# Attention rounds: the first score block moves between the values and the first transposes, the third behind the fourth portion of GEMM products

## The reference

```python
def even_mixer(...):   # layer 0: two kinds of heads, outputs side by side
    o_a, _ = banded_attention(qa, ka, va, slopes_a, 127, 1, sinks)  # 8 heads, softmax over a band
    o_b = stick_breaking_attention(qb, kb, vb)                      # 8 heads, sigmoids and a product
    return concatenate([o_a, o_b]) @ w_out
def odd_mixer(...):    # layer 1: 16 heads, dilated patterns, softmax
def dsa_sparse_attention(...):   # layer 2: 16 heads, softmax over selected keys
```

## Time and profile before

| what | value |
|---|---|
| time, median of 3 (lowest to highest) | 3058.09 us (3057.76 to 3059.72) |
| the profiled execution's own time | 3058.59 us |
| its span | 3056.8 us |
| TensorE busy | 3039.6 us, 99% of the span |
| VectorE, ScalarE, GpSimd busy | 2035.4, 1416.4, 450.1 us |
| stage EV | about 447 to 542 us |
| stage OC | about 1559 to 1652 us |
| stage SX | about 2528 to 2622 us |
| a round of SX, between two starts of first transposes | 11.72 us (2540.14 to 2551.86) |

### The profile page before, as it was taken

One profiled execution on the slowest core, in us unless ns is written; L12 is line 12 of the kernel. 1 busy time (PEld: TensorE's weight loads), 2 busy tenths in 40 slices (PEclk: granted clock), 3 DMA queues, 4 the chain that ended last, 5 costly groups with the idle time before them and its releaser, 6 DMA issues.

```text
span 3056.8 us, 44796 instructions
## 1 busy us (share of the span) xinstructions
PE 3039.6 (99%) x17960; PEld 2621.2 (86%) x17960; DVE 2035.4 (67%) x2896; ACT 1416.4 (46%) x2189; POOL 450.1 (15%) x550
## 2 busy tenths in 40 slices
PE   9999999999999999999999999999999999999999
PEld 8998886887999899988867879998887786789987
DVE  7886258755888478863565757886336876578873
ACT  6444247544444344442455545444236727454442
POOL 1112014212110011101310212110152200031100
PEclk9999999999999999999999999999999999999999
DMA  7763330423774267633232416763332231247732
GB/s 210 175 164 98 102 97 29 146 69 99 193 178 138 97 151 180 162 114 99 88 96 77 152 49 160 178 163 113 86 99 83 79 108 35 76 112 187 170 117 70
DMA packets 287360, 366.93 MB, mean 120 GB/s; under 512 B 12304, under 2 KB 211344, under 8 KB 287024
## 3 DMA queue, kind: packets, MB, share of 16 engines
q1 hardware_dynamic: 233392, 304.42, 31.4%
q0 software_dynamic: 53184, 59.32, 11.9%
q10 hardware_dynamic: 576, 0.33, 0.0%
HBM read 361.92 MB, written 2.10 MB: 119 GB/s over the span
## 4 chain that ended last, share of the span: by engine, by line
PE 94%; issue 3%; POOL 1%; DVE 1%; ACT 1%; POOLq 0%; DVEq 0%; ACTq 0%
PE ps L94 91%; PE ps L97 3%; POOL evQ L142 1%; ACT wh L100 0%; POOL evPb L142 0%; DVE hTl L109 0%; POOL evPa L142 0%; DVE wl L103 0%; DVE xT L103 0%; DVE evQ L115 0%; DVE s_gb L103 0%; POOL rc L103 0%; ACT u_R L100 0%; ACT xn L100 0%; POOL c0ss L103 0%
## 5 line engine op out<-in xcount | busy, mean ns | idle before, releaser
L103 DVE TENSOR_TENSOR wl<-raw,wh 128x1024 fp32r<-128x1024 f32 (+2 forms) x485 | 596.6, 1236 | 498.0 <-ACT wh L100 493.7
L100 ACT ACTIVATE wh<-raw 128x1024 fp32r<-128x1024 f32 (+2 forms) x485 | 504.8, 1049 | 808.7 <-PE ps L94 768.2
L94 PE MATMUL ps<-hTh,wh 128*128 128x256 f32 (+1 forms) x2016 | 671.1, 333 | 2.4 <-DVE wl L103 1.7
L94 PE MATMUL ps<-hTh,wl 128*128 128x256 f32 (+1 forms) x2016 | 666.9, 331 | 0.0
L94 PE MATMUL ps<-hTl,wh 128*128 128x256 f32 (+1 forms) x2016 | 625.0, 331 | 0.2 <-DVE hTl L109 0.2
L94 PEld LDWEIGHTS ps<-hTh,wh 128*128 128x128 f32 x2016 | 383.7, 190 | 44.5 <-issue 9.2
L94 PEld LDWEIGHTS ps<-hTh,wl 128*128 128x128 f32 x2016 | 383.8, 190 | 38.1 <-issue 7.5
L94 PEld LDWEIGHTS ps<-hTl,wh 128*128 128x128 f32 x2016 | 382.6, 191 | 37.4 <-issue 4.7
L100 ACT ACTIVATE wh<-u_raw 128x1024 fp32r<-128x1024 f32 x190 | 201.4, 1062 | 299.9 <-PE ps L94 281.9
L94 PE MATMUL ps<-u_Fh,wl 128*128 128x512 f32 x704 | 273.9, 389 | 0.0
L94 PE MATMUL ps<-u_Fh,wh 128*128 128x512 f32 x704 | 273.9, 389 | 0.0
(11 more groups left out here) (423 smaller groups left out, 6106.3 us busy)
## 6 DMA issues: line engine op xcount, KB each, us to landing
raw<-in_ffn_w_gu SPq DMA_DIRECT2D x118, 512.0 KB, 4.7
raw<-in_ffn_w_down SPq DMA_DIRECT2D x88, 512.0 KB, 3.6
u_raw<-in_ffn_w_gu SPq DMA_DIRECT2D x77, 512.0 KB, 4.9
raw<-in_ffn_w_gu POOLq DMA_DIRECT2D x40, 512.0 KB, 6.1
u_raw<-in_ffn_w_gu POOLq DMA_DIRECT2D x38, 512.0 KB, 6.1
raw<-in_xa_w_kv SPq DMA_DIRECT2D x32, 512.0 KB, 3.7
raw<-in_w_in SPq DMA_DIRECT2D x28, 512.0 KB, 3.6
raw<-in_od_w_in SPq DMA_DIRECT2D x24, 512.0 KB, 3.8
```

The source lines that it names most:

```text
L94: return self.made(lambda e: e.matmul(*a, **k))
L100: return self.made(lambda e: e.activation(*a, **k))
L103: return self.made(lambda e: e.tensor_tensor(*a, **k))
```

## The change

Two calls in TensorE's order move. Nothing else in the program changes: the orders of the other engines, the tiles, the banks, the portions of products and all computed values stay.

```diff
@@ -1244,8 +1244,8 @@
         fill(-1, 3)
         fill(-1, 4)
         for g in range(T_.N):
+            scores(g + 1, 0)
             turn(g, 0, slice(0, 1))
-            scores(g + 1, 0)
             fill(g, 0)
             turn(g, 0, slice(1, None))
             fill(g, 1)
@@ -1257,9 +1257,9 @@
                 turn(g, 1, slice(0, 1))
                 fill(g, 2)
                 turn(g, 1, slice(1, -1))
-            scores(g + 1, 2)
             if g + 1 == T_.N or len(T_.seq[g + 1][0].groups) == 3:
                 fill(g, 3)
+                scores(g + 1, 2)
                 turn(g, 1, slice(-1, None))
             else:
                 turn(g, 1, slice(-1, None))
```

## The result

The changed kernel takes 3069.09 us (median of 6 executions, 3068.51 to 3070.98), the kernel before beside it 3058.38 (6, 3057.76 to 3059.72). The ratio is 1.0036, interval 1.0026 to 1.0046: 10.7 us slower. 3066.1 was forecast, with 3059 to 3072 as the range and 0.77 on "slower". The profiled execution took 3068.58 us, its span is 3066.8.

A forecast was written before the change was run, and what follows sets the result against it. TensorE, busy for 3039.6 of 3056.8 us, was taken as the bound. OC and SX +6.8 and EV +1.6 gave 8.4, said as 8.0, on 3058.1: 3066.1 us, range 3059 to 3072.

The forecast's parts named there:

- The order's saving: TensorE's order in a round: two mode changes for three; head 0's six transposes at 2.01 and not 2.22, saving 0.21.
- first edit: Score block 0 ahead of the first transposes: saves 0.21 by order, but ScalarE's copy comes 1.11 later and a wait appears.
- step from values straight into scores: TensorE at a round's start: entering the score form from values costs between nothing and 0.23; taken as 0.05.
- The wait: Before head 1's transposes: the late copy delays exponentials and division to 5.30, a new wait of 0.79 in every round.
- Rival (a): Only TensorE's own order counts and ScalarE's exponentials hold nothing up: 6 us saved, 3052; chance 0.07.
- the margin: In an OC round, from the first division's end at 4.19 to head 1's transposes at 4.73: 0.54.
- The sum: OC and SX 6.8 plus EV 1.6 give 8.4 us slower; 8.0 said.
- EV, the term that was mis-sized: EV stage: banded rounds 0 to 2 +1.3, round 3 -0.6, stick-breaking rounds 4 to 6 +0.9; +1.6 in all.
- The second edit: Score block 2 behind the fourth portion: saves about 0.1 a round and covers VectorE's late drain of its bank.
- rival (d): The new waits pull the granted clock down, half clock for some 3 us in 14 rounds: 3087; chance 0.07.

The follow-up runs named there:

- e3: Both edits as in the changed kernel, plus two of head 1's four exponentials moved early on ScalarE; 3056.96 us, ratio 0.9995 to the kernel before.
- e10: Both edits as in the changed kernel, plus one of head 1's exponentials moved early on ScalarE; 3062.82 us, ratio 1.0015 to the kernel before.
- e6: Kernel before with score block 2 moved and two GEMM products ahead of the first transposes in rounds 1 to 6 of OC and SX; 3058.84 us.
- after: The changed kernel, with both edits against the kernel before; 3069.09 us, ratio 1.0036.
- e1: Kernel before with only score block 0 moved ahead of the first transposes, score block 2 at its old place; 3074.87 us, ratio 1.0056.
- b1: The kernel before, unchanged and profiled once more; 3057.20 us (one execution).
- e2: Kernel before with only score block 2 moved behind the fourth portion, first transposes right behind the values; 3058.74 us, ratio 1.0001.
- e9: Kernel before with two early exponentials, score block 0 moved in softmax rounds only, score block 2 in OC and SX only; 3055.37 us, ratio 0.9991.
- e8: Both edits and two early exponentials, but score block 0 unmoved in stick-breaking rounds, score block 2 unmoved in OC and SX round 3; 3056.78 us, ratio 0.9996.

## Why the prediction was right, and where its sizes were off

**The order's saving.** 0.21 a round was forecast for the first edit. With the wait taken away (e3), a round is 11.42 and not 11.63: 0.21. The Trainium skill, TensorEngine Tiling (Array Packing), Key Properties, has each change of mode drain TensorE; one change fewer did pay, 0.21 in e3. The step from values straight into scores, taken at 0.05 with 0.23 as its upper end, cost nothing: values to scores is 2.30 (1582.69 to 1584.99), as values to transposes was the earlier trace rows.

**The wait.** The round followed the forecast nearly row by row, from the values' end: ScalarE's copy at 1.76 (forecast 1.81), the division's end at 5.26 (5.30), head 1's transposes at 5.41 (5.36), 0.87 later than score block 1 would let them start (0.79; the profile's own figure for the wait, 0.80, is counted from a modelled end), score block 2 at 7.80 (7.75) without a wait, the values at 9.97 (9.89), the end at 12.27 (12.19). e3 and e10 show that the wait is this chain's. Rival (a) needed a delay under the margin; it was 1.06, for 0.54 by the prediction and 0.39 by e6.

**Who ended the wait.** I wrote that the transposes start 0.06 behind the division, which would be 5.32. They start at 5.41, and for OC and SX the profile names ScalarE's `ocPT` copy, whose merged row ends at 1589.42 + 0.91 = 1590.33, 0.07 earlier. That name misleads. By the kernel's two alternating banks, head 1's first transposes take the bank of head 0's second group, and only the first two of the three copies read it. In a narrower window they end at 1589.42 + 0.64 = 1590.06, 0.34 ahead of the transposes:

```profile
1589.42 0.64 ACT L100 ACTIVATE ocPT<-ps 128x384 f32<-128x384 f32 x2
```

The gaps say the same. In EV of after, each of TensorE's ten waits that a ScalarE instruction ended (`evQ`, `evPT`) ends 0.14 or 0.15 behind that instruction, never 0.07. Head 1's transposes start 0.14 or 0.15 behind the division's end wherever they wait in OC and SX of after, e1 and e10, and 0.15 behind it in the banded rounds, where the last copy had ended 0.52 before. So the division ended the wait, as forecast. What was mis-sized is the step behind it: I took the 0.06 from transposes that follow values, and behind a score block it is 0.15. Why the two differ stays open, and no run moved the copy alone. The waits at the place where I expected them come to 5.6 + 5.6 + 1.9 = 13.1 us, for some 14.

The 5.41 is close to the 5.36 in part by luck: the delay was 0.05 shorter than forecast and the step behind the division 0.09 longer.

**The sum.** 8.4 was added up and 8.0 said, for 10.7 measured. OC and SX lost 4.16 each where 3.4 was forecast. Rounds 1 to 3 lost 0.56 (12.27 for 11.71), rounds 4 to 6 about 0.59 (12.49 for 11.90; the prediction had them at 11.72 too, which they are not), for a forecast of 0.47: some 0.6 of a stage's excess. Of these 0.09 the wait's end gives 0.05 (5.41 for 5.36), and the products between the last transposes and the values 0.04 (1.54 for 1.50). Round 0 and what is left lost 0.7 for 0.6. In its own pieces score block 2 is at 6.21 + 0.93 + 0.69 = 7.83 and not 7.80; transposes that took 0.03 less (0.82 for 0.85, 1590.40 to 1591.22) hide that.

**EV, the term that was mis-sized:** +2.66 for +1.6. Round by round against b1: the banded rounds +0.62, +0.45 and +0.47 (1.5, forecast 1.3); round 3 nothing (13.28 for 13.29), where I had −0.6 for a block moved behind products at half clock, which was an accident of one execution; the stick-breaking rounds +0.48, +0.48 and +0.32 (1.3, forecast 0.9), the last −0.15. I had bounded a stick-breaking round by 0 and 0.5 and taken 0.3; in b1's terms it came out at the upper end. ScalarE's first sigmoid of rounds 4 and 5 starts 2.25 behind the values' end and not 1.75, the 0.50 that I had as the bound. A single profile tells little here, though: against the first profile of before the same four rounds come out at +0.16, +0.48, +0.47 and −0.29.

The two edits can be told apart in round 5, where the wait for `evQ` shrank from 0.99 to 0.30 and two others appeared. The 0.68 before score block 1 is the first edit's: e1 has it, with the 0.99 before score block 2 unchanged, and e2 has not.

```profile
510.96 1.14 PE L94 MATMUL ps<-e_kbT,e_qbT 64*128 64x384 f32 x8 [0.69 <-ACT evQ L100]
```

The 0.66 before the values is the second edit's: e2 has it, beside the 0.29 before score block 2, and e1 has not. It is the old wait in a new place, for 0.30 + 0.66 is 0.96. So EV's loss is the first edit's (e1 alone: 102.30), as in the other stages.

**The second edit.** It was said to save 0.1 and to hide what the first makes late before score block 2. Both are seen: 0.08 in e2, and 2.9 us a stage between e1 and after. Not foreseen: alone, it makes OC's round 4 lose 0.5 (0.4 in SX). In EV it saves nothing (e2 100.04, b1 99.55).

**The clock, rival (d).** With waits of 0.80 in 12.27 us the granted clock of an OC round stayed at 1.00. The Trainium skill, TensorE: Matmul & The Clock Gate, Part 1: The HAM clock gate, has idleness throttle the array; none of the waits in OC did. The one low stretch that I read as agreeing with it does not settle it: the wait of 2.17 ahead of it stands in b1 too, and one of 2.30 in after, and in both the granted clock stayed at 1.00.

## What to carry to other kernels

Before moving a call that another engine's in-order queue starts from, write down two numbers: how late the move makes that queue, and the smallest margin at its far end, counted over data and PSUM banks alike, and less the step from the releaser's end to the start of what it releases. Below the margin the move is free, above it the difference is lost in every round: here 1.06 of delay against 0.39 of margin. A saving in TensorE's own order is real, but it is collected only when the chain that it stretches is shortened in the same change, as in e3 and e9, by their rounds; in the total that gain is at the edge of what can be told. The cure lengthened another queue in its turn (round 4 of e3, 0.6). Hold runs against each other by rounds and not by totals alone: e6 lost in five rounds what it won in one. And before a term is built on a low clock, profile the same kernel twice.

## What the runs showed of the hardware that I had not expected

The half clock in EV's round 3 comes and goes between executions of one program: 0.50 (1.2 GHz) in 488 to 491 in one profile of before, 1.00 (2.4 GHz) in the other, with 1.7 us between the two rounds (15.0 and 13.29). In five of the other profiles (e3, e6, e8, e9, e10) that round took 14.2, 0.9 more, with a granted clock under 1 there as well: in e9 0.50 in 485 to 488 and 0.93 in 488 to 491. In all twelve profiles TensorE had waited 2.17 to 2.30 us for `evQ` just before. What decides it stays open. TensorE's first GEMM product also starts between 7.53 and 9.12 us from profile to profile, with the work ahead of it unchanged. So two single profiles can differ by 2 or 3 us before any edit.
